# The MoE stage of a two-block layer: order of the scatter, the waits of the gate product, and the last down product in column halves

## The reference, cut to what matters

```python
MOE_GROUPS, MOE_EXPERTS_PER_GROUP, MOE_TOPK, MOE_HIDDEN = 4, 8, 2, 256
# top-1 expert group, then top-2 experts inside it; comb holds the weights
for grp in range(MOE_GROUPS):
    h = (jax.nn.silu(jnp.einsum("td,edf->tef", xt, w_gate[grp]))
         * jnp.einsum("td,edf->tef", xt, w_up[grp]))
    out = out + jnp.einsum("tef,efd->td", h * comb[:, grp, :, None], w_down[grp])
...
x = _layernorm(DEEPNORM_ALPHA * x + h, ln_g[i, 1], ln_b[i, 1])
x = x + jax.nn.sigmoid(x @ pe_w_gate[i]) * (p[i].astype(x.dtype) @ pe_w_proj[i])
```

## Time and profile before

| what | value |
|---|---|
| median of 3 runs | 1108.2 us (1104.16 to 1109.47) |
| the profiled execution, its own time | 1104.79 us |
| its span, first to last instruction | 1103.5 us |
| TensorE matmul busy | 94% of the span |
| VectorE / ScalarE busy | 35% / 32% |
| mean of the TensorE clock granted | 0.98 |
| HBM read | 207.12 MB |

### The profile page before, as it was taken

The page is one execution under the profiler, slowest core; times in us unless marked ns, Lnnn a source line. Parts: engine busy times, 40 slices in busy tenths (PEclk is TensorE's granted clock), DMA queues, the critical chain, the costliest instruction groups (busy, mean ns, idle before and its releaser), DMA issues.

```text
span 1103.5 us, 24272 instructions
## 1 busy us (share of the span) xinstructions
PE 1039.6 (94%) x10605; PEld 791.6 (72%) x10605; DVE 381.4 (35%) x946; ACT 353.8 (32%) x1004; POOL 46.1 (4%) x48
## 2 busy tenths in 40 slices
PE   9999999999989998897777799999999999999998
PEld 6777777777766786443333388888888888877787
DVE  2556556656634226110000144532000120065551
ACT  3555555555554322110000123022111341133550
POOL 0110010010010000000000000000000000014000
PEclk9999999999989999999888899999999999999999
DMA  7242232331223685999999943442444434372221
GB/s 282 59 162 107 89 136 91 109 131 70 96 109 135 249 357 215 421 421 421 425 421 423 421 188 136 154 152 101 153 150 152 152 116 151 129 255 77 78 77 39
DMA packets 39742, 209.85 MB, mean 190 GB/s; under 512 B 5056, under 2 KB 14144, under 8 KB 15824
## 3 DMA queue, kind: packets, MB, share of 16 engines
q1 hardware_dynamic: 39632, 208.25, 49.3%
HBM read 207.12 MB, written 1.11 MB: 189 GB/s over the span
## 4 chain that ended last, share of the span: by engine, by line
PE 80%; SPq 9%; DVE 3%; ACT 3%; DMA 3%; issue 2%; POOL 0%; ACTq 0%; DVEq 0%; POOLq 0%
PE ps L2403 12%; PE ps L469 10%; SPq L245 9%; PE ps L2358 5%; PE ps L472 5%; PE ps L2242 4%; PE ps L2752 3%; PE ps L2817 3%; PE ps L797 3%; PE ps L2721 3%; PE ps L808 3%; PE ps L2067 3%; DMA xt<-in_wu 3%; PE ps L1572 2%; PE ps L491 2%; PE ps L525 2%
## 5 line engine op out<-in xcount | busy, mean ns | idle before, releaser
L2403 PE MATMUL ps<-slots,yt 128*128 128x256 f32 x608 | 131.8, 379 | 0.0
L469 PE MATMUL ps<-xt,slots 128*128 128x256 f32 x512 | 128.0, 396 | 0.7 <-issue 0.7
L2403 PEld LDWEIGHTS ps<-slots,yt 128*128 128x128 f32 x608 | 115.4, 190 | 15.6
L469 PEld LDWEIGHTS ps<-xt,slots 128*128 128x128 f32 x512 | 94.7, 194 | 21.0 <-issue 8.9
L1572 PE MATMUL ps<-arena 128*32 128x512 f32 x224 | 53.6, 694 | 13.8 <-DMA slots<-in_wu 9.7
L1572 PE MATMUL ps<-slots,arena 128*32 128x512 f32 x192 | 51.8, 694 | 13.6 <-DMA xt<-in_wu 13.6
L472 PE MATMUL ps<-slots,xt 128*128 128x256 f32 x256 | 63.7, 392 | 0.6 <-issue 0.6
L2358 PE MATMUL ps<-slots,yt 128*128 128x256 f32 x256 | 56.6, 380 | 0.2
L1120 DVE SCALAR_TENSOR_TENSOR arena<-arena 128x256 f32<-128x256 f32 x128 | 56.2, 485 | 0.3
L472 PEld LDWEIGHTS ps<-slots,xt 128*128 128x128 f32 x256 | 46.1, 189 | 10.5 <-issue 4.4
L2358 PEld LDWEIGHTS ps<-slots,yt 128*128 128x128 f32 x256 | 48.1, 190 | 7.1 <-ACT yt L290 0.5
(11 more groups left out here) (407 smaller groups left out, 1738.7 us busy)
## 6 DMA issues: line engine op xcount, KB each, us to landing
slots<-in_wu SPq DMA_DIRECT2D x107, 1024.0 KB, 4.9
arena<-in_wu SPq DMA_DIRECT2D x48, 1024.0 KB, 25.9
extra<-in_wu SPq DMA_DIRECT2D x16, 1024.0 KB, 25.9
yt<-in_wu SPq DMA_DIRECT2D x8, 1024.0 KB, 24.5
xt<-in_wu SPq DMA_DIRECT2D x4, 1024.0 KB, 26.2
arena<-bias_rows SPq DMA_DIRECT2D x1, 2048.0 KB, 14.8
arena<-delta_rows SPq DMA_DIRECT2D x14, 128.0 KB, 7.6
extra<-in_w_vg SPq DMA_DIRECT2D x1, 1056.0 KB, 6.9
```

Source lines behind the costliest of these rows:

```text
L469: q = M.matmul(bank(n, T), self.slots[:, s, k, n * P:(n + 1) * P], self.xt[:, k, :], start=(k == 0), stop=(k == KT - 1))
L2403: q = M.matmul(self.bank(s, UC, t * UC), self.xe[:, k, t * P:(t + 1) * P], self.slots[:, s, k, :], start=(t == 0 and k == 0), stop=(k == K ...
```

## The change

Four edits, all in the MoE stage:

1. `hidden_tensor`: half 0 waits for `xg_a` alone; the wait for `xg_v` stands ahead of half 1.
2. `hidden_tensor`: the scatter of step `i-1` stands between half 0 and half 1, no longer behind half 1.
3. The last four units (u92 to u95, the down weights of step 7) are fetched as eight DMAs of half a megabyte: the low 512 columns of the four, then the high 512 columns of the four. Each row of such a DMA is two pieces of 2 KB per partition where a unit is one piece of 8 KB.
4. The last step has a function of its own, `last_down`: low half of the down product, wait for ScalarE's copy, scatter of the low half into both tiles, then the same for the high half, whose copy is ScalarE's too (`og_b`). `embed_p(2)` comes behind it. VectorE adds and takes statistics by halves of 512 columns: both tiles' low halves, then the high halves.

```diff
--- before.py
+++ after.py
@@ -1390,7 +1390,8 @@
             new("PE", n) for n in ("x_turned_in_banks", "raw_x_turned", "route_sums", "norm_rows_spread", "routed", "counted", "spill_max",
                                    "gathered_low",
                                    "gathered", "weights_turned", "hidden_turned", "down_product", "scattered"))
-        g.first_half = new("PE", "first_tile_scattered")
+        g.half_scattered = [new("PE", f"last_step_scattered{b}") for b in range(2)]
+        g.low_in, g.og_b = new("SP", "last_low_weights_in", 16), new("ACT", "last_high_out_kept")
         (g.var_ln, g.var_exp, g.group_exp, g.top_exp, g.raw_kept, g.scaled, g.xt_kept, g.xg_a, g.silu, g.swt_kept,
          g.ht_kept, g.og_a) = (
             new("ACT", n) for n in ("var_ln", "var_exp", "group_exp", "top_exp", "raw_x_kept", "rows_scaled", "xt_kept",
@@ -1438,9 +1439,10 @@
                 self.hidden_tensor(g, i)
                 self.hidden_scalar(g, i)
                 self.hidden_vector(g, i)
-            self.down(g, i)
-            self.low_out(g, i)
-            self.high_out(g, i)
+            if i < STEPS - 1:
+                self.down(g, i)
+                self.low_out(g, i)
+                self.high_out(g, i)
         self.moe_last_tensor(g)
         self.moe_end_tensor(g)
         self.moe_end_scalar(g)
@@ -1468,8 +1470,17 @@
 
     def moe_sync_rest(self, g):
         SP, I = self.nc.sync, self.ins
-        for u in range(NSLOT + 8, 3 * EXPERTS):
+        last = range(3 * EXPERTS - GRP, 3 * EXPERTS)
+        for u in range(NSLOT + 8, last[0]):
             self.fill(RING[u % NSLOT], U_MOE + u)
+        for b in range(2):
+            for u in last:
+                s = RING[u % NSLOT]
+                part = lambda a: a.rearrange("p (f n) -> p f n", f=2)[:, :, b * 512:(b + 1) * 512]
+                if b == 0:
+                    SP.wait_ge(*self.multiplied[s](self.arrived[s].n // 16))
+                SP.dma_start(part(self.flat(s)), part(I["wu"][U_MOE + u].rearrange("p a b -> p (a b)"))).then_inc(
+                    *(self.arrived[s] if b else g.low_in).up())
         self.fill(4, U_PE + 4)
         for cg, s in enumerate(GATE_SLOTS):
             self.fill(s, U_PE + cg)
@@ -1560,12 +1571,15 @@
 
         M, bank, c, FT = self.nc.tensor, self.bank, self.c, HID // P
         for half in range(2):
+            if half == 1 and i > 0:
+                self.scatter(g, i - 1)
             slots = self.step_slots(i, half)
             if half == 0:
                 M.wait_ge(*g.xg_a(i + 1))
-                M.wait_ge(*g.xg_v(i + 1))
                 if i > 0:
                     M.wait_ge(*g.hm_made(i))
+            else:
+                M.wait_ge(*g.xg_v(i + 1))
             for k in range(KT // 2):
                 for e in range(GRP):
                     r = slice(e * CAP, (e + 1) * CAP)
@@ -1575,8 +1589,6 @@
                     if k == KT // 2 - 1:
                         q.then_inc(*self.multiplied[slots[e]].up())
         g.hidden.append(self.multiplied[slots[GRP - 1]].last())
-        if i > 0:
-            self.scatter(g, i - 1)
         M.wait_ge(*g.sw_made(i + 1))
         if i > 0:
             M.wait_ge(*g.swt_kept(i))
@@ -1626,9 +1638,36 @@
         for b in range(4):
             q = M.matmul(self.bank(4 + b), g.swt[:, b // 2], g.og[:, b % 2 * 512:(b % 2 + 1) * 512], start=(i == 0),
                          stop=True, skip_group_check=True)
-            if b == 1 and i == STEPS - 1:
-                q.then_inc(*g.first_half.up())
         q.then_inc(*g.scattered.up())
+
+    def last_down(self, g):
+
+        M, FT, n = self.nc.tensor, HID // P, STEPS - 1
+        slots = [RING[(12 * n + 8 + e) % NSLOT] for e in range(GRP)]
+        M.wait_ge(*g.low_in(GRP))
+        M.wait_ge(*g.ht_kept(STEPS))
+        for b in range(2):
+            if b == 1:
+                for s in slots:
+                    M.wait_ge(*self.arrived[s](self.multiplied[s].n + 1))
+            for f in range(FT):
+                for e in range(GRP):
+                    r = slice(e * CAP, (e + 1) * CAP)
+                    q = M.matmul(self.ps[r, b, :], g.ht[:, f, r],
+                                 self.flat(slots[e])[:, f * D + b * 512:f * D + (b + 1) * 512],
+                                 start=(f == 0), stop=(f == FT - 1), skip_group_check=True)
+                    if b == 1 and f == FT - 1:
+                        q.then_inc(*self.multiplied[slots[e]].up())
+            if b == 0:
+                q.then_inc(*g.downed.up())
+                M.wait_ge(*g.og_a(STEPS))
+            else:
+                g.down.append(self.multiplied[slots[GRP - 1]].last())
+                M.wait_ge(*g.og_b(1))
+            M.wait_ge(*g.swt_kept(STEPS))
+            for t in range(NT):
+                M.matmul(self.bank(4 + 2 * t + b), g.swt[:, t], g.og[:, b * 512:(b + 1) * 512], start=False, stop=True,
+                         skip_group_check=True).then_inc(*g.half_scattered[b].up())
 
     def moe_scalar(self, g):
         A = self.nc.scalar
@@ -1725,15 +1764,6 @@
             q = V.tensor_scalar(self.xt[:, k, t * P:(t + 1) * P], self.bank(bank, P, (k - 4) * P),
                                 g.lnf[:, row, 0, k:k + 1], g.lnf[:, row, 1, k:k + 1], ALU.mult, ALU.add)
         q.then_inc(*g.xt_kept_v.up())
-
-    def norm_stats(self, g, t):
-
-        V, st = self.nc.vector, g.stats
-        for n in range(2):
-            q = V.bn_stats(st[:, t, 6 * n:6 * n + 6], self.x[:, t, n * 512:(n + 1) * 512])
-        q.then_inc(*g.step.up())
-        V.wait_ge(*g.step.last())
-        V.bn_aggr(st[:, t, 24:26], st[:, t, 0:12]).then_inc(*g.var.up())
 
     def norm_centre(self, g, row, t):
         V, st, x = self.nc.vector, g.stats, self.x[:, t]
@@ -1980,10 +2010,10 @@
     def moe_last_tensor(self, g):
 
 
+        self.last_down(g)
         self.nc.tensor.wait_ge(*g.loaded(1))
         self.nc.tensor.wait_ge(*self.arrived[4](self.multiplied[4].n + 1))
         self.embed_p(g, 2)
-        self.scatter(g, STEPS - 1)
 
     def embed_p(self, g, cg):
 
@@ -2003,7 +2033,11 @@
         self.nc.tensor.wait_ge(*g.xt_kept_v(1))
 
     def moe_end_scalar(self, g):
-        self.nc.scalar.preload_act_table_set("natural_log_exp_and_others")
+        A = self.nc.scalar
+        self.low_out(g, STEPS - 1)
+        A.wait_ge(*g.down[STEPS - 1])
+        A.activation(g.og[:, 512:], self.bank(1), ACT.Copy).then_inc(*g.og_b.up())
+        A.preload_act_table_set("natural_log_exp_and_others")
         for t in range(NT):
             self.norm_scalar(g, 1, t)
             self.norm_kept_scalar(g, 1, t, 4 + 2 * t)
@@ -2012,19 +2046,33 @@
         V = self.nc.vector
         V.wait_ge(g.spill_over.sem, 1)
 
-        def add(t):
-            V.wait_ge(*(g.scattered(STEPS) if t else g.first_half(1)))
-            x = self.x[:, t].rearrange("p (a n) -> p a n", a=2)
-            V.scalar_tensor_tensor(x, x, ALPHA, self.ps[:, 4 + 2 * t:6 + 2 * t], ALU.mult, ALU.add).then_inc(
-                *g.step.up())
+        st = g.stats
+
+        def add(t, half):
+
+            V.wait_ge(*g.half_scattered[half](t + 1))
+            x = self.x[:, t, half * 512:(half + 1) * 512]
+            V.scalar_tensor_tensor(x, x, ALPHA, self.bank(4 + 2 * t + half), ALU.mult, ALU.add).then_inc(*g.step.up())
             V.wait_ge(*g.step.last())
 
-        add(0)
-        self.norm_stats(g, 0)
+        def stats(t, half):
+            V.bn_stats(st[:, t, 6 * half:6 * half + 6], self.x[:, t, half * 512:(half + 1) * 512]).then_inc(*g.step.up())
+
+        def variance(t):
+            V.wait_ge(*g.step.last())
+            V.bn_aggr(st[:, t, 24:26], st[:, t, 0:12]).then_inc(*g.var.up())
+
+        for t in range(NT):
+            add(t, 0)
+            stats(t, 0)
+        add(0, 1)
+        stats(0, 1)
+        variance(0)
+        add(1, 1)
         self.norm_centre(g, 1, 0)
-        add(1)
+        stats(1, 1)
+        variance(1)
         self.norm_kept_vector(g, 1, 0, 5)
-        self.norm_stats(g, 1)
         self.norm_centre(g, 1, 1)
         self.norm_kept_vector(g, 1, 1, 7)
         for t in range(NT):
```

## The result

The changed kernel takes 1101.27 us (median of 8 runs, 1099.29 to 1104.77) against 1107.97 (8 runs, 1104.16 to 1109.47); the ratio is 0.995 with a 95% interval from 0.9932 to 0.9968. That is faster by 3.5 to 7.5 us. The forecast was 1103.2, 5.0 us less than before.

The account below looks back on a forecast made before the run. The MoE's weight stream and TensorE's order were taken as the bound. Last high halves landing at 621.8 plus a 10.9 us tail put the gate at 632.7, not 637.63: 5.0 us off 1108.2 gives 1103.2 us, range 1099.0 to 1107.5.

Parts of the forecast that it names:

- What bounds it: MoE stage: weight stream and TensorE's order end it almost together; the rest of the program moves with the embedding gate's start.
- Edit 1, 1.5 us: Step 0: half 0 starts without VectorE's rows, so the first fill and the weight stream come 1.5 us earlier.
- Edit 2: Step 7: the 3.64 us scatter falls into the wait between the halves; half 1 takes 3.5 us at full clock.
- The reason given for the full clock: Step 7: only 2 us idle ahead of half 1, like the earlier gap of some 1.9 us that cost nothing.
- with edit 2 alone the down product could gain only the 1.1 us until 622.0 lands: Step 7: with only the scatter moved, the last down product still waits for the last unit's landing, gaining 1.1 us.
- Edit 3, pieces at 88 ns: Last four units: 2 KB pieces cost 88 ns each, 11.3 us in place of 9.94, so 1.3 us more.
- free: Rival for the last four units: 2 KB pieces cost nothing extra, gain 5.9 to 6.3 us, 1102.1 us; chance 0.15.
- dear: Rival for the last four units: 2 KB pieces cost 102 ns, gain 3.1 to 3.2 us, 1105.0 us; chance 0.10.
- Edit 4, the tail at 10.9 us from H: Tail: high down product, copy wait, scatter, embedding products and transposes take 10.9 us from H to the embedding's gate.
- H: Landing of the last units' high column halves, forecast at 621.8 us against 622.0 for the last unit before.
- The sum: Embedding gate starts at 632.7 in place of 637.63: 4.9, rounded to 5.0 us; median 1108.2 becomes 1103.2 us.
- The rival in which the clock falls in the tail: Tail: TensorE's short pieces with 0.9 us waits lower its clock; the gain goes, at worst 1116.7 us; chance 0.05.

Follow-up runs that it names:

- e2: Kernel before, with only the scatter moved between the two halves of the gate product: ratio 1.0011, 200.47 us from first fill to gate.
- e9: e4 with 16 more identity matmuls, read by nothing, in TensorE's wait behind the last transposes of step 7: ratio 0.9992, 198.92 us from first fill to gate.
- e4: Changed kernel with the last four units loaded whole, down product still in column halves: ratio 1.0018, 202.37 us from first fill to gate.
- second pair of traces: Kernel before and changed kernel, each run again unchanged: ratios 1.0003 and 0.9933, 198.74 and 195.12 us from first fill to gate.
- e6: Changed kernel with half 0 again waiting for both halves of the rows: ratio 0.9963, 195.20 us from first fill to gate.
- e7: Changed kernel with the last four units fetched in column quarters, pieces of 1 KB: one run, 1102.72 us.
- e8: Changed kernel run again, unchanged, against the kernel before: ratio 0.9933, 195.12 us from first fill to gate.
- e10: Changed kernel with 5 and 3 idle identity matmuls in TensorE's waits ahead of the first gather: 1100.47 us, ratio 0.9941.
- e3: Kernel before with only the last units and the last step's work in column halves, scatter and half 0's waits as before: ratio 1.0006.
- e11: Second run of the kernel before with only half 0's wait for VectorE's rows moved to half 1: ratio 0.9993.
- e1: First run of the kernel before with only half 0's wait for VectorE's rows moved to half 1: ratio 1.0004.

## Why the prediction was right

**What bounds it** (right). The rest moved as one piece with the start of the gate, to 0.1 us in 14 traces.

**Edit 1, 1.5 us.** Right in mechanism and size: 1.55 us by the first fill, at the same clock. The step left out the first gather's own clock, which takes 1.3 to 1.5 us, and once 2.9 (e2), of an execution in which it is low; the changed kernel's profile is one, which is why its own stage became only 4.2 us shorter.

**Edit 2.** Right for the changed kernel: idle time ahead of half 0 of step 7, half 0 at the lower clock, half 1 at the full one, 3.65 us for the 3.5 assumed. The reason given for the full clock, a wait of 2 us ahead of half 1 like one that cost nothing, wasn't put to the test there: half 0 waited 7.62 us for its weights, not some 6, ended later, and left a wait of 0.41 us. Half 1 had the full clock in all eight traces with edit 2, behind waits of 0.19 to 2.29 us, the longest in e9. Wrong is the step "with edit 2 alone the down product could gain only the 1.1 us until 622.0 lands": it loses 1.4 (e2). The landing was right; the term that failed is the length of the down product behind it, 3.64 us assumed and 6.09 measured. The prediction looked at the clock in the halves of step 7 and in the tail, and never at a down product that waits for its last weights.

**Edit 3, pieces at 88 ns.** 84.7 measured, and 10.83 us for the four units where the sum had 11.3. It lies nearer the lower of the bounds (78 and 102 ns). The rivals "free" and "dear" are out. The Trainium skill (DMA: Bandwidth & Descriptors, Specifications) gives 512 B as the smallest transfer at line rate; here 8 KB pieces run at 310 ns (2.485 us for 128 pieces on 16 engines), 2 KB ones at 84.7 and 1 KB ones at 47, which is 92% and 82% of the rate of the 8 KB ones. For pieces of 1 and 2 KB these traces don't bear the page out, and the measured rates decide.

**What the halves are worth** was told too small. The prediction named them for their earlier landing; without them the changed kernel is 7.4 us longer behind the fill (e4), 3.5 of it by the clock (e4 against e9).

**Edit 4, the tail at 10.9 us from H.** 10.87. VectorE's path stayed beside it. The margin of the low path was 0.24 us and not 1.0: the high half landed 0.5 us earlier than the sum had it, and the low product and its scatter took 1.92 and 1.99 us by the records for 1.82 and 1.73.

**The sum.** At equal clocks in the gather: 1.55 from the start of the stream, 4.1 from the rest (199.04 to 194.96), 5.6 us against the forecast of 5.0; with the second pair of traces (198.74 to 195.12) 5.2. The runs, 3.5 to 7.5 us faster, can't tell these apart. The 0.5 too much for the pieces is most of the 0.6 between forecast and first pair. The rival in which the clock falls in the tail didn't come in the changed kernel, nor in any variant with halves and edit 2 (e6, e7, e8, e10); where TensorE waited 4.8 or 4.9 us for u95 ahead of the down product it did come (e4, e2), so the rival named the right danger at the wrong place.

## What to carry to other kernels

Where a stage ends with a weight stream, taking work off TensorE's path helps only as far as the last landing, and can harm: the wait it opens may cost the clock for the work behind it, as in e2. Cut the last transfer so that a part of the work, with its copy and its scatter, can be done before the last landing, and move the work at the same time; neither change gained anything alone (e2, e3). When spans of single executions vary more than the change, compare the stage between two instructions whose surroundings are unchanged.

## What the runs showed of the hardware

- The TensorE clock was at 0.50 for the 8.2 us that followed 5.8 us with 0.42 us of work (e4), and at 1.00 in the same place when matmuls of no use brought the work to 4.16 of 6.1 us (e9). Work without a purpose gave back 3.5 us; each kernel has one trace.
- The same kernel gets either clock in the first gather (3.84 us in e11, 5.19 in e1), behind waits of 1.3 and 0.8 us. The Trainium skill (TensorE: Matmul & The Clock Gate, Part 1: The HAM clock gate) says that the phase of the clock's control is free-running, so that one kernel runs a different number of matmuls at the lower clock from run to run; the two traces of one kernel agree.
- A DMA piece cost some 9 ns beyond its bytes, by an estimate from 310 ns for 8 KB (before), 84.7 for 2 KB (changed kernel) and 47 for 1 KB (e7).
